# Upward strips as one 512-column product per step, the row factor at the residual, and second-tile masks written by ScalarE

## What is computed

```python
# first block: mixer (two kinds of attention), cross attention, then
a = jnp.square(jax.nn.relu(rms_norm(h, g_mlp) @ w_up))   # w_up 1024 x 4096
h = h + a @ w_down                                       # w_down 4096 x 1024
# second block: projections, compressed, selected, windowed and dilated attention, gates, then
h2 = _rmsnorm(x, norm2_g)
x = x + jnp.square(jax.nn.relu(h2 @ w_up_2)) @ w_down_2
# its attention (heads of 64 columns)
s = jnp.where(mask, s, NEG); p = softmax(s)
```

## Time and profile before

| | us |
|---|---|
| time, median of 3 runs | 876.5 (876.34 to 876.64) |
| span of the profiled execution | 874.3 |
| TensorE busy in it | 865.4 (99%) |
| GpSimd busy | 679.1 (78%) |
| VectorE busy | 458.7 (52%) |
| ScalarE busy | 429.2 (49%) |
| MLP1, from the first product of up 0 to the end of down 7 | about 235 to 420 |
| MLP2, the same | about 690 to 871 |

### The profile page before, as it was taken

One profiled execution on the slowest core, in us unless ns is written; L12 is line 12 of the kernel. 1 busy time (PEld: TensorE's weight loads), 2 busy tenths in 40 slices (PEclk: granted clock), 3 DMA queues, 4 the chain that ended last, 5 costly groups with the idle time before them and its releaser, 6 DMA issues.

```text
span 874.3 us, 13275 instructions
## 1 busy us (share of the span) xinstructions
PE 865.4 (99%) x5362; PEld 753.0 (86%) x5362; DVE 458.7 (52%) x666; ACT 429.2 (49%) x590; POOL 679.1 (78%) x389
## 2 busy tenths in 40 slices
PE   9999999999999999999999999999999999999998
PEld 7898887898899999998887797777788899999996
DVE  5697652423444221335788899559955552323233
ACT  6674486366354443343763645636455454434430
POOL 3789473958679999988898879812638889999881
PEclk9999999999999999999999999999999999999999
DMA  9865352534545666654854554520224446566531
GB/s 336 337 218 195 121 192 96 192 122 145 169 168 184 203 199 215 210 191 147 295 169 133 174 177 140 187 84 1 97 98 143 161 153 216 195 196 216 198 110 49
DMA packets 65555, 149.22 MB, mean 171 GB/s; under 512 B 4801, under 2 KB 10977, under 8 KB 65377
## 3 DMA queue, kind: packets, MB, share of 16 engines
q1 hardware_dynamic: 65504, 148.53, 50.8%
HBM read 147.47 MB, written 1.05 MB: 170 GB/s over the span
## 4 chain that ended last, share of the span: by engine, by line
PE 87%; DVE 6%; POOL 2%; ACT 2%; DMA 2%; issue 1%; SPq 0%; ACTq 0%; DVEq 0%
PE ps L1878 75%; PE ps L2059 2%; POOL w_lo L680 2%; PE ps L2033 2%; PE ps L1971 1%; PE ps L2045 1%; DMA h<-in_x 1%; PE ps L2305 1%; DVE xn L1768 1%; DVE arena L1321 1%; PE ps L2223 1%; PE ps L2244 1%; DMA raw<-in_w_in 1%; PE ps L2167 1%; PE ps L2012 0%
## 5 line engine op out<-in xcount | busy, mean ns | idle before, releaser
L680 POOL TENSOR_TENSOR w_lo<-raw,w_hi 128x512 fp32r<-128x512 f32 (+2 forms) x364 | 667.2, 1870 | 140.9 <-ACT w_hi L723 140.8
L723 ACT ACTIVATE w_hi<-raw 128x1024 fp32r<-128x1024 f32 (+3 forms) x193 | 247.8, 1321 | 255.4 <-PE ps L1878 119.4
L1878 PE MATMUL ps<-w_hi,x_hi 128*128 128x512 f32 (+1 forms) x672 | 266.8, 397 | 1.3 <-POOL w_lo L680 1.1
L1878 PE MATMUL ps<-w_hi,x_lo 128*128 128x512 f32 (+1 forms) x672 | 259.9, 387 | 0.0
L1878 PE MATMUL ps<-w_lo,x_hi 128*128 128x512 f32 (+1 forms) x672 | 259.8, 387 | 0.0
L1878 PE MATMUL ps<-x_hi,w_hi 128*128 128x256 f32 x704 | 201.7, 287 | 0.0
L1878 PE MATMUL ps<-x_hi,w_lo 128*128 128x256 f32 x704 | 199.3, 283 | 0.0
L1878 PE MATMUL ps<-x_lo,w_hi 128*128 128x256 f32 x704 | 199.2, 283 | 0.0
L1878 PEld LDWEIGHTS ps<-w_hi,x_hi 128*128 128x128 f32 x672 | 126.3, 188 | 33.4 <-issue 6.5
L1878 PEld LDWEIGHTS ps<-w_hi,x_lo 128*128 128x128 f32 x672 | 126.2, 188 | 25.8
L1878 PEld LDWEIGHTS ps<-w_lo,x_hi 128*128 128x128 f32 x672 | 126.4, 188 | 22.3
(11 more groups left out here) (285 smaller groups left out, 818.0 us busy)
## 6 DMA issues: line engine op xcount, KB each, us to landing
raw<-in_w_up SPq DMA_DIRECT2D x32, 1024.0 KB, 5.4
raw<-in_w_down SPq DMA_DIRECT2D x32, 1024.0 KB, 4.8
raw<-in_w_in SPq DMA_DIRECT2D x31, 1024.0 KB, 5.3
raw<-in_w_xkv SPq DMA_DIRECT2D x8, 1024.0 KB, 5.1
raw<-in_w_out SPq DMA_DIRECT2D x8, 1024.0 KB, 4.9
raw<-in_w_xq SPq DMA_DIRECT2D x4, 1024.0 KB, 5.1
raw<-in_w_xo SPq DMA_DIRECT2D x4, 1024.0 KB, 4.9
raw<-in_w_in SPq DMA_DIRECT2D x6, 512.0 KB, 7.9
```

The costliest lines, as they stand in the source:

```text
L680: x = nc.gpsimd.tensor_tensor(LO[s % 2][:, 2048 * q + d0:2048 * q + d1], RAW[n % 3][:, d0:d1], HI[s % 2][:, 2048 * q + d0:2048 * q + d1].b ...
L723: nc.scalar.activation(HI[s % 2][:, 2048 * q + c0:2048 * q + c1], RAW[n % 3][:, c0:c1], ACT.Copy).then_inc(hi_done, 1)
L1878: last = T.matmul(dst, l, r, start=start and i == 0, stop=stop and i == 2, skip_group_check=w_stationary)
```

## The change

An upward step becomes two products: the high weights by the high and the low activations side by side (512 columns, a whole bank), and the low weights by the high activations (256 columns, the first half of the same bank). The strip thus ends with two halves in each of four banks: up 0 in banks 0 to 3, every other in banks 4 to 7. Their sum is made outside TensorE: ScalarE copies the second halves to `act_c` (`up_second`), VectorE adds the first halves, and ScalarE does relu, square and the rounded high part (`up_square`). The low part stays with VectorE. The row factor is no longer broadcast: since relu and the square go through a positive factor, its square is multiplied at the residual. In the 18 attention units of tile 1 (all but those of the first two) the mask is written to the banks by a ScalarE copy (`seed`), which comes after the exponentials of the unit two before, and the two identity products go.

```diff
+            def seed(n):
+                act.wait_ge(ex_done, n - 1)
+                sc = scores_of(n)
+                m = units[n]["mask"][1].unsqueeze(1).unsqueeze(1).broadcast_to(list(sc.shape))
+                nc.scalar.activation(sc, m, ACT.Copy).then_inc(seeded, 1)
...
+            def up_second(base, a0, j):
+                act.wait_ge(strip_done, up_strip(base, j) + 1)
+                src = bank(up_bank(j), 4).rearrange("p (c x) -> p c x", c=4)[:, :, S:2 * S]
+                nc.scalar.activation(act_c.rearrange("p (c u) -> p c u", u=S), src, ACT.Copy).then_inc(up_taken, 1)
+
+            def up_square(base, a0, j, abuf, before):
+                act.wait_ge(up_evac, a0 + j + 1)
+                link(nc.scalar.activation(act_c, act_q, ACT.Relu))
+                link(nc.scalar.activation(act_q, act_c, ACT.Square))
+                act.wait_ge(strip_done, down_strip(base, j - 2) + 1 if j >= 2 else before)
+                c = slice(1024 * (j % 2), 1024 * (j % 2) + 1024)
+                nc.scalar.activation(XH[abuf][:, c], act_q, ACT.Copy).then_inc(a_hi, 1)
+
             def mlp(base, a0, abuf, before):
+                j = 0
                 for i in range(2, 16):
-                    hi(base + i)
-                    for j in range(8):
-                        if up_strip(0, j) == i - 2:
-                            ...
+                    hi(base + i, 0)
+                    if j and i - 3 == up_strip(0, j - 1):
+                        up_square(base, a0, j - 1, abuf, before)
+                    hi(base + i, 1)
+                    if j < 8 and i - 2 == up_strip(0, j):
+                        up_second(base, a0, j)
+                        j += 1
+                up_square(base, a0, 7, abuf, before)
...
             def activate(...):                            # VectorE
-                V.scalar_tensor_tensor(act_q..., bank(4 + 2 * (j % 2), 2)..., 0.0, bc(rB...), ALU.max, ALU.mult)
-                V.tensor_tensor(act_q, act_q, act_q, ALU.mult).then_inc(sq_ready, 1)
+                dve.wait_ge(up_taken, at(n, 2))
+                V.tensor_tensor(act_q..., bank(up_bank(j), 4)...[:, :, 0:S], act_c..., ALU.add).then_inc(up_evac, 1)
                 dve.wait_ge(a_hi, at(n, 2))
                 V.tensor_tensor(XL[abuf][:, c], act_q, XH[abuf][:, c].bitcast(f32), ALU.subtract).then_inc(a_lo, 1)
...
+            def both(dst, xb, k, wh, wl, start, stop):    # TensorE, one upward step
+                hl = xb.rearrange("p (z k u) -> p z k u", z=2, u=S)
+                T.matmul(dst, wh, hl[:, :, k, :], start=start, stop=stop, skip_group_check=True)
+                return T.matmul(dst[:, 0:S], wl, hl[:, 0, k, :], start=False, stop=stop, skip_group_check=True)
...
                         if m == "up":
-                            if d["j"] >= 2 or ups[0] >= 8: pe.wait_ge(up_evac, at(ups[0] - 1, 2))
+                            if d["j"] >= 2: pe.wait_ge(up_evac, at(ups[0], 2))
...
                 filled_strip(s0)
-                strip(s0 + 1, 0, 12)
-                broadcast_rstd(bank(0))
-                strip(s0 + 1, 12)
-                pe.wait_ge(rb_taken, bcasts[0])
+                strip(s0 + 1)
                 strip(s0 + 2)
```

More of the change, by code:

```diff
@@ L95, in build @@
         LO = [sb(f"w_lo{i}", [P, 4096], f32r) for i in range(2)]
-        XH = [sb(f"x_hi{i}", [P, 2048], f32r) for i in range(2)]
-        XL = [sb(f"x_lo{i}", [P, 2048], f32r) for i in range(2)]
+        XB = [sb(f"x{i}", [P, 4096], f32r) for i in range(2)]
+        XH, XL = [x[:, 0:2048] for x in XB], [x[:, 2048:4096] for x in XB]
         xn = sb("xn", [P, NT, D])
@@ L424, in build, with up_bank @@
         MLP_TURNS = FF // 512 // 2 - 1
+        def up_bank(j):
+            return 0 if j == 0 else 4
         def up_strip(base, j):
@@ L533, in scores_of @@
             return half.rearrange("p r (s w) -> p r s w", w=units[n]["w"])
+        SEEDED = [n for n in range(U_A + 2, NU) if units[n]["t"] == 1]
         NORMS = ["g_mix", "g_mem", "g_cross", "g_mlp", "g_final", "norm1_g_2", "norm2_g_2"]
@@ L1029, in _ @@
                 exps(n)
+                if n + 2 in SEEDED:
+                    seed(n + 2)
                 if n - U_A in (1, 2):
@@ L1169, in scaled_copy, with residual @@
                 V.tensor_tensor(hg[:, t, c], h[:, t, c], gbuf[0][:, c], ALU.mult).then_inc(hg_ready, 1)
-            def residual(s, gain):
+            def residual(s, gain, scale=None):
                 r = BANKED.index(s)
@@ L1176, in residual @@
                     bank_wait(r, b)
-                    x = V.tensor_tensor(h[:, t, c], h[:, t, c], bank(b), ALU.add)
+                    if scale is None:
+                        x = V.tensor_tensor(h[:, t, c], h[:, t, c], bank(b), ALU.add)
+                    else:
+                        x = V.scalar_tensor_tensor(h[:, t, c], bank(b), rstd_n[:, 2 * scale + t:2 * scale + t + 1],
+                                                   h[:, t, c], ALU.mult, ALU.add)
                     if gain is None:
@@ L1500, in mlp @@
                 for j in (0, 1):
-                    activate(j, up_strip(base, j) + 1, a0, abuf)
+                    activate(j, a0, abuf)
                 if base == MLP1:
@@ L1508, in mlp @@
                     for j in (2, 3):
-                        activate(j, up_strip(base, j) + 1, a0, abuf, i)
+                        activate(j, a0, abuf, i)
             mlp(MLP1, 0, 0)
-            residual(IN2 - 1, g45)
+            residual(IN2 - 1, g45, 3)
             for b in range(4):
@@ L1845, in _ @@
             row_scale(6)
-            broadcast_rstd(6, bank(0))
+            square_rstd(6)
             mlp(MLP2, 8, 1)
-            residual(NS - 1, None)
+            residual(NS - 1, None, 6)
         @block.tensor
@@ L1919, in strip @@
                         pe.wait_ge(a_lo, at(a_n[0], 2))
-                b0 = 4 + 2 * (d["j"] % 2) if m == "up" else d.get("pair", 0)
+                b0 = up_bank(d["j"]) if m == "up" else d.get("pair", 0)
                 for n_step, (o, k) in enumerate(steps[first:last]):
@@ L1932, in strip @@
                                   hi_[:, c:c + w], lo_[:, c:c + w], k == 0, k == KT - 1, False)
-                    elif m in ("T", "up"):
+                    elif m == "up":
+                        c = 2048 * (k // 4) + w * (k % 4) + P * o
+                        x = both(bank(b0 + o), XB[d["x"]], k, hi_[:, c:c + P], lo_[:, c:c + P], k == 0, k == KT - 1)
+                    elif m == "T":
                         c = 2048 * (k // 4) + w * (k % 4) + P * o
@@ L2018, in unit_loop @@
                         u = units[i]
-                        if i >= 2:
+                        if i in SEEDED:
+                            pe.wait_ge(seeded, SEEDED.index(i) + 1)
+                        elif i >= 2:
                             pe.wait_ge(ex_done, i - 1)
                         sc, per, mask = scores_of(i), len(u["segs"]) // 2, u["mask"]
-                        if mask is not None:
+                        if i not in SEEDED:
                             c, m = mask
@@ L2031, in unit_loop @@
                                 for x, (q, kk) in enumerate(qk):
-                                    first = mask is None and k == 0 and x == 0
-                                    last = T.matmul(sc[:, r, k, :], q, kk, start=first, stop=x == len(qk) - 1,
+                                    last = T.matmul(sc[:, r, k, :], q, kk, start=False, stop=x == len(qk) - 1,
                                                     skip_group_check=True)
```

42 lines of the change are left out of this document (20 added, 22 removed).

## The result

The changed kernel takes 897.8 us (median of four executions, 888.3 to 902.5), the kernel before 876.6 (876.3 to 877.0). The ratio of the medians is 1.024, and it is 1.020 (interval 1.015 to 1.026) without the longest execution, which counts as slow. The forecast was 884.5, with a range of 878 to 889. The sign was right. The time was not: only the shortest execution lies in the range, and it is the one that was profiled. So there are two questions: what this execution lost, and why the others lost 6 to 14 us more.

What follows compares the result with a forecast made beforehand. The prediction took TensorE's stream of matmuls as the bound (busy 865.4 of 874.3 us). +5.3 + 5.5 - 4.9 - 1.3 + 3.4 = +8.0 gave a span of 882.3, and 2.2 around it 884.5 us, range 878 to 889.

Steps and rivals of the forecast that it cites:

- The sign: Whole kernel: slower, 884.5 us against 876.5; chance of slower by over 0.2% put at 0.87.
- Part 2, ScalarE's queue: Before down 0: square waits behind a rounding that awaits raw data; down 0 starts 5.3 us later in MLP1, 5.5 in MLP2.
- With the wait it was 2.14 there, and at most 4.64 + 1.07 = 5.7: VectorE's low part before down 0: duration including its wait for GpSimd's instruction, in us; 2.1 was taken.
- ScalarE becomes the bound: Rival, attention units: ScalarE's mask copies delay exponentials that TensorE's transposes wait for; 5 to 10 us more, 890 to 895; chance 0.05.
- Part 5, the clock: After TensorE's idle gaps before down 0: clock falls, costing 1.7 us at each of two gaps, 3.4 lost.
- The rival in which the clock stays up: Gaps before down 0 occur but TensorE's clock does not fall: 881.1 us; chance 0.27.
- Part 1, the merged product: Upward strips: a step of one 512- and one 256-column product saves 0.0127 us, 0.41 per strip.
- the two pieces: Merged product's operand in two pieces 2048 apart: might cost what the merge saves; 889.4 us, little-gain rival, chance 0.05.
- Only 12 strips count: Both MLPs: gains before down 0 are worth nothing, only up 2 to up 7 count; 12 x 0.41 = 4.9 us saved.
- Part 3, later strips: Strips after the first: no stall expected; a possible 2.3 us at down 7 was kept only in the range.
- Part 4, the masks: Attention units of tile 1: ScalarE copies replace identity products, 1.9 us less 0.6 given back, 1.3 saved.

Runs made afterwards that it cites:

- square0: Changed kernel with the first upward strip's clip and square moved ahead of the third strip's weight rounding in ScalarE's queue, both MLPs: 870.6 us, ratio 0.993.
- after_turn: Changed kernel with GpSimd waiting at one place in each MLP until VectorE's subtraction of the first activations is done: 888.4, 888.6, 887.8 and 888.8 us.
- psum0: Changed kernel with the first upward strip's square written to PSUM, so VectorE's subtraction has one SBUF operand: 886.2, 888.3, 885.8 and 887.4 us.
- busy_turn: after_turn plus 60 and 76 products of zeros on TensorE between up 1 and down 0 of the two MLPs: 884.8 us.
- onepiece: Changed kernel with the merged product's moving operand as one piece of 512 adjacent columns in place of two pieces of 256: single execution 895.7 us.
- noseed: best with all masks written by TensorE again, none by ScalarE: 871.6 us, ratio 0.994.
- best: square0 with GpSimd waiting for VectorE at the first three subtractions of each MLP: 870.2 us, ratio 0.992 against the kernel before.

## Why the prediction was right or wrong

**Part 2, ScalarE's queue: right in mechanism and place.** Down 0 of MLP1 was forecast at 264.6 and started at 264.59, and square0 shows that the place in the queue makes both gaps. In MLP2 +5.5 was forecast and +7.6 measured. The rounding came 1.1 later than the shift of the whole would put it (718.00, against 712.66 + 4.2), as its data landed later, and the low part took 3.07 in place of 2.1. The idle times were 5.9 and 8.2, not 6.6 and 6.7: up 1 ended later than forecast (down 0 could have followed at 258.5, not 258.0), mostly since the merged product gained less.

**The step that failed** is in the same part: "With the wait it was 2.14 there, and at most 4.64 + 1.07 = 5.7". This took it that VectorE gets in when GpSimd's current instruction ends. The trace of before shows nothing else, and in the changed kernel's first trace that was so some fifty times; once an end that came 0.04 us after VectorE's start was missed (L1597, at 447.0). But VectorE may lose its turn, and in five traces it then lost all that followed until GpSimd paused; for the subtraction of 1.2 us this made 8.3, 9.0, 14.0 and 18.8 us. Where the low part is what TensorE waits for, all of this counts, and the clock falls further. Six of the eight executions of the changed kernel were 5 to 14 us above the shortest; of the eight in after_turn and psum0, none was over 2.5 above theirs. The range ended at 889 for want of this case. Of the executions of the changed kernel above 889 one was traced (893.7), and its lost turns, with the low clock behind them, account for all that it took more; that those of 895 to 902 us are the same, more often or at other lines, is inferred from the eight without spread. Rival "ScalarE becomes the bound" would have covered part of the times, for another reason; no trace shows it.

**Part 5, the clock: right.** 1.7 per gap was forecast; the profiled execution lost 2.0 and 1.5. The rival in which the clock stays up is busy_turn (884.8 against 888.5), and it didn't happen by itself. With waits of 5.9 and 6.3 us, the low clock cost as much as 2.6 and 2.9 (after_turn).

**Part 1, the merged product: the size was off by half.** 0.0127 per step was forecast, 0.41 a strip. Measured: 11.29 against 11.51, 0.22 a strip, 0.007 a step. The mis-sized term is the merged product: 0.2271 was taken from a downward strip, and beside products of 256 columns it is 0.23 to 0.24. The doubt of the forecast, the two pieces, cost nothing (onepiece). "Only 12 strips count" was right for the changed kernel. 12 x 0.22 less the 0.03 that each of 12 downward strips loses is 2.3 in place of 4.9.

**Part 3, later strips: right.** Every later pair of strips takes 22.23 us; in this trace there are no stalls at the other downs, down 7 among them. A lost turn can make one there as well: 8.0 us in square0, 2.6 in noseed.

**Part 4, the masks: right.** 1.3 was forecast; the trace shows 1.2, noseed 1.1.

**Not foreseen: 0.8 at about 500 us.** The kernel before waits there for an instruction of VectorE with two operands in SBUF, which took 2.04 us for two. In best (second line) it takes 1.12:

```profile
499.92 2.04 DVE L1693 TENSOR_TENSOR gain<-gain,small 15x192 f32<-15x192 f32 x2
```

```profile
498.04 1.12 DVE L1740 TENSOR_TENSOR gain<-gain,small 15x192 f32<-15x192 f32 x2
```

The traces show GpSimd there, met at another phase. In all three kernels the second of the two instructions ends 0.21 us after an end of one of GpSimd's low-part subtractions: in the kernel before it began beside one of 512 columns (ended 501.75, VectorE 501.96), in the changed kernel and in best beside one of 164 (506.71 and 506.92; 498.95 and 499.16). No run changed this alone.

In numbers, forecast and profiled execution: down 0 later +10.8 and +12.9; clock +3.4 and +3.5; strips -4.9 and -2.3; masks -1.3 and -1.2; 500 us 0 and -0.8. The sums are +8.0 and +12.1, and the spans differ by 12.2. The rest up to the median of 897.8 is put down to VectorE's lost turns, as said above.

## What to carry to other kernels

Before a step is handed to another engine, write down that engine's queue at the place: here the arithmetic moved well, and one rounding that stood ahead of it and waited for its data cost 18 us (shortest executions compared), which one move gave back. A VectorE instruction on two SBUF operands whose result TensorE waits for should not meet a GpSimd queue without pauses: put one operand in PSUM, or stop GpSimd for it. And take the spread of a kernel's executions as data: when they differ by 1 to 2%, one profile is not the kernel.

## What was not expected of the hardware

- VectorE and GpSimd exclude each other here when both read two operands in SBUF; VectorE mostly gets in at the next end of an instruction. But it can be passed over at two, four or five ends in a row, and was then let in only when GpSimd's queue paused, 1.1 us before its own end (four traces; a fifth with an instruction of half the size, L1221 in onepiece, so it isn't tied to the line that was changed). What decides it stays open. The one trace of the kernel before has no such case, though it has the same kinds of instructions, and the longest of its 30 executions is 1.9 us above the shortest.
- After 5.9 us of idleness in the middle of the kernel the granted clock is at the lower level (1.2 GHz) for part of the next windows (0.78, 0.81) and then back at 1.00. Products of zeros in the gap keep it at 1.00 throughout.
- In these 32-bit products, one of 512 columns is followed by the next after 0.227 in a row of its like and after 0.237 on average where one of 256 comes next (up 2 of MLP1), and the product of 256 there after 0.117, in place of 0.120 among its like. Two pieces 2048 columns apart read as fast as one.
